# Later modulations streamed by single chunks through four quarters, and the second scan's first decay and rate made two tiles later

## What is computed

```python
sh1, sc1, gt1, sh2, sc2, gt2 = ada_mod(c, ada_w, ada_b)      # silu(c) @ w + b: 1024 -> 6 * 1024, also for c_ctx
h = modulate(rms_norm(x, norm1_g), sh1, sc1)                  # 768 tokens: 256 of ctx, 512 of x
p = h @ w_in
o_gdn  = gdn_mixer(p_gdn, ...)      # first scan: gated delta rule, 4 heads of 128, both directions
o_rwkv = rwkv7_mixer(p_rwkv, ...)   # second scan: 8 heads of 64, both directions
#   w_pre = w0 + tanh(xw) @ w2;  log_w = -exp(-softplus(-w_pre) - 0.5)    the decay
#   a = sigmoid(a0 + xa @ a2)                                             the rate
x = x + gt1 * (concat(o_gdn, o_rwkv) @ w_out)
x = x + gt2 * peer_ffn(modulate(rms_norm(x), sh2, sc2), ...)  # gathered experts
# then the second model: pooling mixer + convolutional feed-forward, attention + feed-forward,
# each with six modulations made from ada_w_2 of its layer
```

## Time and profile before

| what | value |
|---|---|
| median of 3 runs | 4079.0 us (4072.67 to 4080.2) |
| the profiled execution | 4074.47 us, its span 4071.8 us |
| TensorE busy | 3577.0 us, 88% of the span |
| VectorE busy | 2603.9 us, 64% |
| GpSimd busy | 1207.0 us, 30% |
| ScalarE busy | 1025.4 us, 25% |
| mean granted clock of TensorE | 0.949 of full speed |
| later modulations, first to last chunk in the first scan | 242.8 to 522.7 us |
| second projection, first to last tile | 542.9 to 720.4 us |

### The profile page before, as it was taken

How to read it: one execution, slowest core, us unless ns; L and a number is a source line. 1 busy time by engine, 2 the same in 40 slices (tenths; PEclk the granted TensorE clock), 3 DMA queues, 4 the chain that set the end, 5 groups by cost and what they waited for, 6 DMA issues and landing times. The chain is left out here.

```text
span 4071.8 us, 54603 instructions
## 1 busy us (share of the span) xinstructions
PE 3577.0 (88%) x21557; PEld 2137.6 (52%) x21557; DVE 2603.9 (64%) x4972; ACT 1025.4 (25%) x2744; POOL 1207.0 (30%) x1197
## 2 busy tenths in 40 slices
PE   7988899899996999777777777679999999999998
PEld 4555665798865544233233333255555444548863
DVE  4856534767745667677677675566666667637765
ACT  2432222444312233333332323330000011511000
POOL 1033300434410333433333333223232420014442
PEclk8999899889988999999999999989999999999999
DMA  4156520000024999999999999721111431012233
GB/s 170 42 208 238 198 83 21 10 2 3 3 78 145 399 415 419 420 420 420 420 420 420 420 420 421 329 67 62 62 61 73 163 146 67 1 42 83 83 127 142
DMA packets 183884, 786.65 MB, mean 193 GB/s; under 512 B 13062, under 2 KB 75793, under 8 KB 108624
## 3 DMA queue, kind: packets, MB, share of 16 engines
q0 software_dynamic: 77408, 550.32, 32.8%
q1 hardware_dynamic: 105072, 230.76, 16.1%
q10 hardware_dynamic: 1152, 2.10, 0.1%
HBM read 781.03 MB, written 2.10 MB: 192 GB/s over the span
## 5 line engine op out<-in xcount | busy, mean ns | idle before, releaser
L2532 PE MATMUL bank<-row,dg 128*128 128x512 f32 x1444 | 699.4, 625 | 208.3 <-ACT dg L2641 206.7
L2734 DVE CUSTOM_DVE_ANT_0 row<-row,bank 128x1024 f32<-128x1024 f32 x361 | 440.9, 1221 | 297.9 <-DMA row<-in_experts,idxs 278.8
L2532 PEld LDWEIGHTS bank<-row,dg 128*128 128x128 f32 x1444 | 275.4, 198 | 596.4 <-issue 583.1
L2800 POOL DMA_INDIRECT row<-in_experts,idxs x361 | 348.0, 964 | 625.6 <-PE bank L2532 560.1
L2532 PE MATMUL bank<-wring,dg 128*128 128x512 f32 x604 | 288.0, 610 | 70.6 <-ACT dg L2641 67.9
L104 PE MATMUL bank<-hT,wring 128*128 128x256 f32 (+1 forms) x864 | 286.7, 492 | 12.4 <-DVE be L1991 8.7
L3496 DVE TENSOR_TENSOR pad<-pad,bank 128x256 f32<-128x256 f32 (+2 forms) x396 | 154.1, 413 | 191.8 <-PE bank L104 184.6
L2632 ACT ACTIVATE act<-dots 128x2 f32<-128x2 f32 x256 | 52.0, 203 | 818.9 <-DVE dots L2734 815.2
L2734 DVE CUSTOM_DVE_ANT_0 wring<-wring,bank 128x1024 f32<-128x1024 f32 x151 | 184.4, 1221 | 110.2 <-DMA wring<-in_experts,idxs 101.8
L2532 PEld LDWEIGHTS bank<-wring,dg 128*128 128x128 f32 x604 | 112.8, 194 | 230.4 <-issue 223.5
L104 PEld LDWEIGHTS bank<-hT,wring 128*128 128x128 f32 x864 | 166.0, 193 | 128.6 <-issue 101.4
(11 more groups left out here) (601 smaller groups left out, 6669.3 us busy)
## 6 DMA issues: line engine op xcount, KB each, us to landing
wring<-in_ada_w SPq DMA_DIRECT2D x36, 2048.0 KB, 8.6
wring<-in_ffn_w_down SPq DMA_DIRECT2D x50, 1024.0 KB, 7.0
wring<-in_ffn_w_up SPq DMA_DIRECT2D x44, 1024.0 KB, 7.7
wring<-in_peer_w_query SPq DMA_DIRECT2D x16, 1024.0 KB, 7.9
wring<-in_w_in SPq DMA_DIRECT2D x7, 2048.0 KB, 8.3
wring<-in_attn_w_qkv SPq DMA_DIRECT2D x3, 2048.0 KB, 8.0
row<-in_experts,idxs POOLq DMA_INDIRECT x361
wring<-in_ffn_w_down SPq DMA_DIRECT2D x10, 512.0 KB, 4.0
```

The lines of the kernel that those rows point to most:

```text
L2532: ins = e.matmul(ks[half], self.dg[u % 4], self.places[self.slot[u]][:, 1024 + half * 512:1536 + half * 512], start=(x == 0), stop=(x == 127))
L2734: e.tensor_tensor_reduce(row, row, P.pairs[g % 2], 1.0, 0.0, MUL, ADD, self.dots[:, g % 2, x:x + 1]).then_inc(*V.up("pg_dot", j))
L2800: e.indirect_dma_start(self.places[r], None, P.i["experts"], bass.IndirectOffsetOnAxis(ap=idu[:, b, j % 128:j % 128 + 1], axis=0)).then_in ...
```

## The change

Three things are changed. Groups 1 to 8 of the later modulations are loaded by `stream`, in 64 DMAs of one chunk each, into four quarters (halves of the two slots, in turn) with a semaphore for each quarter. Chunk m is issued when TensorE has spent chunk m-4; the first four are issued when the slots' last holders are free. TensorE's new `rows_pe` makes the same products in the same order, waits for each chunk by itself, and marks the two slots free at chunks 61 and 63. Group 0 stays with the old functions. In the second projection the first decay and rate are made after tile i=9 in place of i=7; ScalarE's two steps of the head move from i=9 and 10 to i=10 and 11, VectorE's from i=8 and 9 to i=10 and 11, and its last from i=11 to i=12. TensorE's use of the operands stays at i=13.

```diff
@@ class LaterMods
+        self.lq = [P.flag(f"later_landed{q}", 16) for q in range(4)]
+
+    def quarters(self, who):
+        P = self.P
+        one, two = P.weight(who, 1, WSLOT), P.weight(who, 1, WSLOT)
+        return (one[0], two[0]), [w[:, 0, h * 2048:(h + 1) * 2048] for _, w in (one, two) for h in range(2)]
+
+    def stream(self, sy):
+        P = self.P
+        slots, place = self.quarters("sy")
+        for m in range(64):
+            g, c, q = 1 + m // 8, m % 8, m % 4
+            if m >= 4:
+                sy.wait_ge(*P.at("later_spent", m - 4))
+            elif q % 2 == 0:
+                sy.wait_ge(*P.at("wfree", slots[q // 2] - 2))
+            wv = (P.i["ada_w_2"][g // 3 - 1] if g >= 3 else P.i["ada_w"][0]).rearrange("(c p) n -> p c n", p=128)
+            sy.e.dma_start(place[q], wv[:, c, g % 3 * 2048:(g % 3 + 1) * 2048]).then_inc(*self.lq[q].up("later_row", m))
+
+    def rows_pe(self, pe):
+        P, e = self.P, pe.e
+        slots, place = self.quarters("pe")
+        for m in range(64):
+            g, c, q = 1 + m // 8, m % 8, m % 4
+            if c == 0:
+                pe.wait_ge(*P.at("silu", g // 3 > 0))
+                k = P.own(pe, 7, "later", g)
+            pe.wait_ge(*P.at("later_row", m))
+            for j in range(4):
+                ins = e.matmul(k[32 * j:32 * j + 32, :], P.sc[g // 3 > 0][:, c, :], place[q][:, j * 512:(j + 1) * 512],
+                               start=(c == 0), stop=(c == 7))
+            ins.then_inc(*self.T.up("later", g, c))
+            self.T.mark("later_spent", m)
+            if m >= 60 and q % 2:
+                self.T.mark("wfree", slots[q // 2])
+            yield 1
+            if c == 7:
+                self.turn(pe, g)
+                yield 1
@@ class GdnScan
     def sy(self, sy):
-        for n in range(4, 36):
-            self.P.later.sy(sy, n)
+        self.P.later.stream(sy)
@@ GdnScan.pe
-        mods = P.later.pe(pe, range(1, 9))
+        mods = P.later.rows_pe(pe)
@@ RwkvProject.pe
-            if i == 7:
+            if i == 9:
                 pe.wait_ge(*P.at("x3"))
                 P.rscan.decay_pe(pe, 0)
                 P.rscan.rate_pe(pe, 0)
@@ RwkvProject.ac
-            if i in (9, 10):
+            if i in (10, 11):
                 next(head)
@@ RwkvProject.dv
-            if i in (8, 9):
+            if i in (10, 11):
                 next(head)
-            if i == 11:
+            if i == 12:
                 dv.wait_ge(*P.at("rl_out", 3))
                 for _ in head:
                     pass
```

## The result

| | before | after |
|---|---|---|
| median of 4 runs each, alternating | 4075.84 us (4066.37 to 4080.2) | 4019.72 us (4011.24 to 4026.05) |
| ratio, 95% interval | | 0.9864 (0.9836 to 0.9892) |
| the same pair on a later occasion: 25 and 8 runs | 4061.28 us (4039.62 to 4079.52) | 4019.89 us (4013.45 to 4038.97) |
| ratio, 95% interval | | 0.9914 (0.9883 to 0.9945) |
| profiled execution, its span | 4074.47, 4071.8 us | 4023.99, 4021.9 us |

What follows compares the result with a forecast made beforehand. TensorE was taken as the bound, held up by late loads in the first scan and a bank wait in the projection; 16.0 + 6 + 11.1 = 33 us off 4074.5 gave 4041.5, plus 4.5 for the median 4046, range 4035 to 4065.

Steps and rivals of the forecast that it cites:

- Part 1, the waits: First scan, quarter loads: all seven TensorE waits for `ada_w` loads go, 16.0 us, at least 10.
- Part 1, the landing of 1 MB: First scan: a 1 MB load takes 5.2 us from issue to landing, between 3.5 and 7.5.
- The shortest distance of 7.8 us: First scan: least time from chunk m-4's end to TensorE's readiness for chunk m; holds even for a 7.5 us load.
- Part 1, the clock: First scan: fuller clock in five half-speed stretches totalling 26.7 us gives back 6 us, between nothing and 11.3.
- Part 2: Second projection, decay and rate after tile 9: the 8.71 us bank wait and 2.4 us of slow clock go, together 11.1.
- the two covers: Second projection: spare time before TensorE would wait, 5 us for banks at tile 12, 5.7 us for the operands.
- The ring of banks: Second projection: tile 9 needs banks 2 and 3, held by decay and rate until VectorE's late read; costs 8.71 us.
- (1): First scan: TensorE waits for VectorE or ScalarE where the loads stood; gain only 14 us, 4065; chance 0.12.
- (2): Second projection: the bank wait only moves to tile 12 or the operands at i=13; 4055 to 4057; chance 0.08.
- (3): First scan: the queue serves 1 MB loads one after another, 5.2 us each; slower, 4100; chance 0.03.
- The sum's last sentence: Stages after the projection, including the second scan, only start earlier; no gain or loss of their own was counted.
- The step from the profiled execution to the median, 4.5 us, and the range: Whole kernel: 4.5 us added to the profiled forecast 4041.5, giving median 4046; range 4035 to 4065.

Runs made afterwards that it cites:

- read_first: Kernel before, with VectorE's read of decay and rate at i=8 put ahead of that tile's norm; ratio 1.0001 (0.9979 to 1.0024).
- before_later_by_3: Kernel before, with six of projection tile i=10's products made twice, so TensorE reaches the second scan 2.6 us later; ratio 1.0013 (0.9988 to 1.0037).
- the parts: Against the kernel before: quarter loads alone, decay and rate left after tile 7, 0.9945; decay and rate after tile 9 alone, old 2 MB loads, 0.9961.

## Why the prediction was wrong, by its own steps

- **Part 1, the waits.** Right. 16.0 us were to go whole, all seven, and none for a load is left. The waits for VectorE grew by 2.2 us, "issue" by 1.5 and those for GpSimd by 0.5; the prediction had put such a return under the clock's term. That distance is what counts is shown by the kernels with m-2 and m-3: 22.4 and 4.0 us of waits.
- **Part 1, the landing of 1 MB.** Mis-sized and without effect. 5.2 us were taken, between 3.5 and 7.5; measured were 4.7 to 9.7 with a median of 6.5 at distance four, 5.0 at distance two. Up to three more are under way at distance four. The shortest distance of 7.8 us was thus less safe than it looked: the chunk used at 280.23 was sent for at 272.2 and landed 7.3 us later, 0.7 us before its use. The one new wait at a chunk, 1.6 us before 317.87 and put down to "issue", is not for its load, which went out at 305.6 and landed 5.5 us later:

```profile
317.87 1.07 PE L606 MATMUL bank<-wring,sc 128*32 128x512 f32 x8 [1.58 <-issue]
...
L562 SPq DMA_DIRECT2D wring<-in_ada_w x1: 328/328/328, 305.6 to 305.6; - x1
...
DMA to landing us min/median/max: 5.5/5.5/5.5
```

  Of the rule on the fixed 2.0 us a DMA (the Trainium skill, DMA: Bandwidth & Descriptors, Anatomy of one DMA), the formula gives 4.4 us for 1 MB, an estimate from that page, beside the 4.7 of the quickest load. The page fitted it to loads that GpSimd issues, which the prediction did not say; SyncE issues these. That the fixed part is not paid one after the other is shown by the 64 loads' stretch, 256.9 us or 4.0 us a chunk, less than the 4.7 of the quickest.
- **Part 1, the clock.** 6 us were taken, net of what returns as waits; measured were 11.1 us less busy time and 4.1 more of other idle time, 7.0 net. The sum came out, its two parts were not told apart: the low level stood for more time than the five stretches of 26.7 us, some 39 us before and some 10 after (twice what 0.93 and 0.98 miss from 1, over 279.9 and 256.9 us).
- **Part 2.** Right: 11.1 us forecast, 11.3 measured, and the two covers within 0.3 us of what they were given. The ring of banks is shown by `read_first`.
- **Rivals 1, 2 and 3** fall in the same rows: no wait for VectorE in the place of the loads' (1), no wait at tile 12 or 13 (2), and loads that overlap (3).
- **The sum's last sentence: "Later stages wait for their own forerunners, so they only start earlier."** This step failed. It put any change of the later stages' own length at nothing. The second scan did not only start earlier, it took 15.3 us less in the profile, with the same products and the same idle time, because the clock fell in it in other places and for less time (0.93 granted against 0.89). That the kernel before can have the changed kernel's pattern is shown by `before_later_by_3`; what picks the pattern stays open.
- **The step from the profiled execution to the median, 4.5 us, and the range.** This failed too. The profiled execution was forecast at 4041.5 and took 4024.0, 17.5 us less, 15.3 of them in the second scan; then 4.5 us were added for the median, which for the changed kernel lies 4.3 below its profiled execution. Together that is the 26 us between 4046 and 4019.7. The result lies 15.3 us under the range: with the second scan as long as before it would have been just at its edge. The range took the scatter of before from three runs (4072.67 to 4080.2) and gave 4.5 us for it; over 77 runs it is 48 us. Against a before whose runs all lay near its upper end, a gain of 35 us was measured as 56; the forecast gain of 33 lies well inside the longer comparison's 22 to 48. With half of those 48 us in place of the 4.5, the range would have reached some 20 us lower, to about 4015.
- **Of the clock's price** the Trainium skill (TensorE: Matmul & The Clock Gate, Part 1) says half of the throttled time. In the second scan the rows agree: from 0.89 of 347.1 us to 0.93 of 331.8 the time at the low level goes from about 76 us to 46, twice what is missing from 1, and 15.3 us were won by 30. In the chunks they agree in part: from 0.93 to 0.98 the low time fell by some 29 us, and TensorE's busy time by 11.1 where half would be 14.5; some of the low time was idle time. Of the 11.1 us 7.0 reached the stretch's length. The prediction's 6 stood against the 13.4 by that page; the busy time lies nearer to the page's number, the net gain nearer to the prediction's.

What stays open: how much of the second scan's difference belongs, on the average, to the change. The ratios of the parts, 0.9945 and 0.9961, allow anything from nothing to some 10 us beside the 23 and 11 of their own stretches. What picks the clock's pattern in an execution is open too: order, delay and chip were not varied one by one over enough profiles.

## What to carry to other kernels

When an in-order queue waits for its loads though the bandwidth is not used up, look at how many pieces of work lie between a load's release and its use, and split the buffers until that time is longer than a load under the load's own traffic; smaller loads at the old distance give nothing. A producer that takes banks from a ring long before its reader comes blocks the ring for everyone: put it late enough that its reader is the next thing to run. And before a gain under 1% is forecast or judged, find out how much the same kernel differs from itself: here it was 48 us on 4060, nearly all of it going with the clock, and four runs of it can lie on one side.

## What the runs showed of the hardware

- The same instructions on TensorE, with the same idle time, took from 324.9 to 358.6 us, as the granted clock was 0.95 to 0.85 over them, in fourteen profiles of one execution each. The five whose clock first fell 0.3 to 0.5 us after their start took 331.7 or 331.8 us, the two at 1.0 us 327.9, the two at 2.2 us 332.1, and the three at -0.6 us between 347.1 and 358.6.
- In the changed kernel TensorE's clock stood at 0.50 for the 16 us from 721.9 on, though TensorE was busy in all of them. In the 20 us before, with the clock at 0.91 on the average, it had been busy for 15.56, in short pieces. A long wait ahead of the scan did not bring it on either: with 7.2 us put back into the projection the scan behind it was the shortest in the profiles, 324.9 us.

```profile
701.00:721.00 20.00, 15.56 (x433) 13.78 (x434) 14.55 (x25) 7.84 (x20) 12.27 (x19) 0.91 0.01 2
```

- A 1 MB load landed after 5.0 us at the median with at most two chunks let out at a time, and after 6.5 with at most four, from the same queue; in the changed kernel a load issued with no other under way took 4.7 to 5.0 us, one with two others under way 6.3 to 9.7.
